# Moving one of two 31-tap convolutions from VectorE to GpSimd, in a two-block transformer kernel

## The reference

```python
hl = modulate(rmsnorm(xl, g_pre_mix[i]), ml[0], ml[1])
zl = hl @ w_in[i]
...
def conformer_branch(z, dw_w, dw_b, ln_g, ln_b):
    a, g = jnp.split(z, 2, axis=-1)
    u = a * jax.nn.sigmoid(g)
    u = depthwise_conv(u, dw_w) + dw_b      # 31 taps, 256 channels, padding 15 on both sides
    u = layernorm(u, ln_g, ln_b)
    return jax.nn.silu(u)
...
merged = jnp.concatenate([rmsnorm(attn, ...), rmsnorm(conf, ...), rmsnorm(sc, ...)], axis=-1)
return merged @ w_o
```

## Time and profile before

| | |
|---|---|
| median of 3 runs | 1858.12 us (1856.57 to 1863.64) |
| the profiled execution, its own time | 1859.7 us |
| its span, first to last instruction | 1857.9 us |
| busy: PE, PEld | 1657.9 us (89%), 1433.6 us (77%) |
| busy: DVE, ACT, POOL | 1235.8 us (67%), 486.9 us (26%), 469.3 us (25%) |
| POOL's hi splits (L1925) | 364 of 128x1024, mean 1291 ns |
| DVE's taps of the two convolutions (L1697) | 120, 84.1 us |

### The profile page before, as it was taken

How to read it: one execution, slowest core, us unless ns; L and a number is a source line. 1 busy time by engine, 2 the same in 40 slices (tenths; PEclk the granted TensorE clock), 3 DMA queues, 4 the chain that set the end, 5 groups by cost and what they waited for, 6 DMA issues and landing times.

```text
span 1857.9 us, 27002 instructions
## 1 busy us (share of the span) xinstructions
PE 1657.9 (89%) x10974; PEld 1433.6 (77%) x10974; DVE 1235.8 (67%) x1668; ACT 486.9 (26%) x1009; POOL 469.3 (25%) x368
## 2 busy tenths in 40 slices
PE   6889589999787899999887979999999797889997
PEld 6876379999687799998654748888888485679996
DVE  7752358887677788868975364444444697568886
ACT  3323212111350412213246251111011513641111
POOL 2200124443232344422200301212121040124442
PEclk9989799999898899999899989999999898989999
DMA  7445655555464555554200203232323041035651
GB/s 263 144 148 167 236 202 174 180 180 181 159 222 164 193 179 181 175 178 159 91 23 1 81 21 114 91 102 90 102 90 101 23 135 58 31 95 177 180 176 54
DMA packets 69876, 247.28 MB, mean 133 GB/s; under 512 B 7456, under 2 KB 10528, under 8 KB 69664
## 3 DMA queue, kind: packets, MB, share of 16 engines
q1 hardware_dynamic: 69792, 246.18, 41.2%
HBM read 245.10 MB, written 1.05 MB: 132 GB/s over the span
## 4 chain that ended last, share of the span: by engine, by line
PE 56%; DVE 31%; ACT 6%; issue 6%; POOL 1%; DMA 0%; SPq 0%; DVEq 0%; POOLq 0%; ACTq 0%
PE psum L319 12%; PE psum L321 12%; PE psum L320 12%; DVE lo_ring L294 9%; DVE relu L1125 4%; DVE c_conf L1697 3%; DVE hid_lo L1126 3%; PE psum L335 3%; PE psum L337 2%; PE psum L336 2%; PE psum L953 2%; DVE x L1088 1%; PE psum L409 1%; POOL hi_ring L1925 1%; DVE normed L1086 1%
## 5 line engine op out<-in xcount | busy, mean ns | idle before, releaser
L1925 POOL TENSOR_SCALAR hi_ring<-raw_ring 128x1024 fp32r<-128x1024 f32 x364 | 469.1, 1291 | 1362.1 <-PE psum L321 674.0
L294 DVE TENSOR_TENSOR lo_ring<-raw_ring,hi_ring 128x1024 fp32r<-128x1024 f32 x364 | 545.8, 1501 | 92.6 <-POOL hi_ring L1925 59.8
L319 PE MATMUL psum<-x_hi,hi_ring 128*128 128x256 f32 (+1 forms) x1424 | 448.2, 315 | 24.1 <-DVE lo_ring L294 24.0
L320 PE MATMUL psum<-x_lo,hi_ring 128*128 128x256 f32 (+1 forms) x1424 | 442.6, 311 | 0.0
L321 PE MATMUL psum<-x_hi,lo_ring 128*128 128x256 f32 (+1 forms) x1424 | 442.4, 311 | 0.0
L319 PE MATMUL psum<-hid_hi,hi_ring 128*128 128x256 f32 (+1 forms) x1024 | 315.8, 308 | 4.1 <-DVE hid_lo L1126 4.1
L321 PE MATMUL psum<-hid_hi,lo_ring 128*128 128x256 f32 (+1 forms) x1024 | 313.7, 306 | 0.0
L320 PE MATMUL psum<-hid_lo,hi_ring 128*128 128x256 f32 (+1 forms) x1024 | 312.7, 305 | 0.0
L319 PEld LDWEIGHTS psum<-x_hi,hi_ring 128*128 128x128 f32 x1424 | 276.2, 194 | 44.3 <-DVE lo_ring L294 30.1
L320 PEld LDWEIGHTS psum<-x_lo,hi_ring 128*128 128x128 f32 x1424 | 276.2, 194 | 13.4 <-issue 0.2
L321 PEld LDWEIGHTS psum<-x_hi,lo_ring 128*128 128x128 f32 x1424 | 275.8, 194 | 13.1
(11 more groups left out here) (373 smaller groups left out, 1889.5 us busy)
## 6 DMA issues: line engine op xcount, KB each, us to landing
raw_ring<-weights SPq DMA_DIRECT2D x460, 512.0 KB, 4.1
h_const<-hyb_consts SPq DMA_DIRECT2D x1, 1088.0 KB, 11.6
x<-xT SPq DMA_DIRECT2D x1, 1024.0 KB, 5.8
x<-ctxT SPq DMA_DIRECT2D x1, 1024.0 KB, 17.1
outT<-x SPq DMA_DIRECT2D x1, 1024.0 KB, 4.8
shared<-shared_consts SPq DMA_DIRECT2D x1, 398.0 KB, 13.8
par<-params SPq DMA_DIRECT2D x1, 301.5 KB, 6.4
```

The source lines that it names most:

```text
L294: nc.vector.tensor_tensor(lo_ring[:, u % SPLIT_SLOTS, :], raw_ring[:, UNIT_AT[u] % RAW_SLOTS, :], hi_ring[:, u % SPLIT_SLOTS, :].bitcast(F ...
L319: nc.tensor.matmul(bank(u % BANKS, T), w_hi, hi[:, k, 0:T], start=(k == 0), stop=False)
L320: nc.tensor.matmul(bank(u % BANKS, T), w_hi, lo[:, k, 0:T], start=False, stop=False)
L1925: nc.gpsimd.tensor_scalar(hi_ring[:, u % SPLIT_SLOTS, :], raw_ring[:, slot, :], 1.0, 0.0, ALU.mult, ALU.add).then_inc(hi_ready, 1)
```

## The change

Plane 1's taps leave DVE and go to POOL, in both layers; plane 0 and the third branch stay. [...] POOL first rounds all units up to base+7, waits until DVE has written plane 1 of `c_u`, and then does three taps, one hi split, three taps, and so on, until the 31 are done: ten groups of three, and one of a single tap. DVE takes 3 taps a unit in place of 5 or 4, and 2 after each of the last three lo splits in place of 6. Waits are added: DVE's for its own memset of the pads, and PE's "mean" and DVE's "center" wait for `pool_taps`.

```diff
+    c_tap = r("c_tap", [P, 2, TB])
...
+    POOL_TAPS = [3, 3]
...
             if step == "mean":
                 pe.wait_ge(flag("branches_done"), l + 1)
+                pe.wait_ge(flag("pool_taps"), l + 1)
...
-        link(nc.vector.memset(c_u[:, :, :, PAD + SEQ:], 0.0))
+        nc.vector.memset(c_u[:, :, :, PAD + SEQ:], 0.0).then_inc(flag("pads_set"), 1)
+        dve.wait_ge(flag("pads_set"), l + 2)
...
-                    taps.extend((conf_tap, i, k) for k in range(CONF_K))
+                    taps.extend((conf_tap, i, k) for k in range(CONF_K if i == 0 else 0))
...
-                do_taps(4 if l else 5)
+                do_taps(3)
...
             if step == "center":
                 dve.wait_ge(flag("conf_mean_ps"), l + 1)
+                dve.wait_ge(flag("pool_taps"), l + 1)
...
+            do_taps(2)
+            if i == 2:
                 branch_dve("taps")
-            do_taps(6)
...
+            def tap(L, j):
+
+                T, S = L.T, L.S
+                parts = lambda ap: ap.rearrange("p (s t) -> p s t", s=S)
+                acc, source = parts(c_conf[:, 1, 0:T]), c_u[:, 1, 0:S, j:j + SEQ]
+                w = pcol("conf_w", (2 * L.l + 1) * CONF_K + j)
+                if j == 0:
+                    link(nc.gpsimd.tensor_scalar(acc, source, w, pcol("conf_b", 2 * L.l + 1), ALU.mult, ALU.add))
+                    return
+                product = parts(c_tap[:, j % 2, 0:T])
+                link(nc.gpsimd.tensor_scalar(product, source, w, None, ALU.mult))
+                last = nc.gpsimd.tensor_tensor(acc, product, acc, ALU.add)
+                if j < CONF_K - 1:
+                    link(last)
+                else:
+                    last.then_inc(flag("pool_taps"), 1)
+
+            u = 0
+            for L in LAYERS:
+                a1 = L.base + ORDER.index("a1")
+                while u <= a1 + SPLIT_SLOTS:
+                    hi_split(u)
+                    u += 1
+                wait_drained(pool, a1)
+                j = 0
+                while j < CONF_K:
+                    for _ in range(min(POOL_TAPS[L.l], CONF_K - j)):
+                        tap(L, j)
+                        j += 1
+                    hi_split(u)
+                    u += 1
+            while u < UNITS:
+                hi_split(u)
+                u += 1
```

More of the change, by code:

```diff
@@ L253, in program @@
     consts_set, split_hi, x_ready = sem("consts_set"), sem("split_hi"), sem("x_ready")
-    pe_step, act_step, dve_step = sem("pe_step"), sem("act_step"), sem("dve_step")
+    pe_step, act_step, dve_step, pool_step = sem("pe_step"), sem("act_step"), sem("dve_step"), sem("pool_step")
     flags = {}
@@ L1919, in _, with hi_split @@
         def _(pool):
-            for u in range(UNITS):
+            link = Link(pool, pool_step)
+            def hi_split(u):
                 slot, turn = UNIT_AT[u] % RAW_SLOTS, UNIT_AT[u] // RAW_SLOTS
```

## The result

| | before | changed |
|---|---|---|
| median | 1859.87 us (4 runs, 1856.57 to 1863.64) | 1928.79 us (4 runs, 1927.2 to 1930.4) |
| ratio | | 1.0353, 95% interval 1.0332 to 1.0375 |
| span of the profiled execution | 1857.9 us | 1926.6 us |

The change makes the kernel 3.5% slower, 66 us by the ratio, 68.9 us between the medians and 68.7 us between the two spans. The forecast was 1902 us (+44) with a range from 1857 to 1932. The direction and the path were right, the size was a third too small.

A forecast was written before the change was run, and what follows sets the result against it. PE was taken to set the pace in layer 0's input projection, DVE just keeping up, with waits for `c_kl` before the kv units. 27 (layer 0) + 20 - 3 (layer 1) = 44 us on 1858.1 gave 1902 us, range 1857 to 1932.

The forecast's parts named there:

- The path: Input projection: hi splits queued behind three POOL taps delay base+16's lo split, `c_kl` and the kv unit, through nine groups.
- POOL's price of a tap: Product, addition and two waits on POOL: 1.85 us a tap in layer 0, 1.15 us in layer 1.
- Rival C: POOL dearer than thought (weight from memory, wait for itself, two inputs through one port): 1930 to 1960 us; chance 0.11.
- Contention: DVE instructions in POOL's way, each at full time less 0.2 us: 26.1 us in layer 0, 18.5 in layer 1.
- The sum in layer 0: POOL alone 59.5 us plus 26.1 of DVE in its way; kv unit at 947 instead of 920.0, +27 us.
- What comes back in layer 1: Leftover taps behind `rotate(0)` go, ahead of the first maximum: -3 us.
- The clock: PE's granted clock falls in its pauses, mostly beside POOL's and DVE's pace: nothing added, some 5 us at the upper end.
- Rival A: POOL and DVE run side by side, so no exclusion time is added: 1857 us, no change; chance 0.10.
- B: Faster: POOL and DVE side by side and low prices, a 4.2 us group, PE setting the pace: 1843 us; chance 0.07.
- D: Cheap POOL taps with the exclusion between POOL and DVE as it is: 1864 to 1880 us; chance 0.12.

The follow-up runs named there:

- experiment 4: The changed kernel with one POOL tap ahead of each hi split from base+8 to base+20 and the other 18 behind them; a single execution took 1928.6 us.
- experiment 1: The changed kernel with POOL's product in six forms by tap number (constant or memory weight, one or two operations, flat operands); a single execution took 1920.8 us.
- experiment 2: The changed kernel without 30 of plane 0's 31 taps on DVE, left out in each layer; a single execution took 1920.0 us.
- the cheap form: The changed kernel with a second operation, + 0.0, in every product on POOL; 1911.1 us, ratio 1.0251 to the kernel before.

## Why the prediction came out as it did

**The path** (a hi split behind three taps, the lo split of base+16, `c_kl`, the kv unit): right, and shown by experiment 4, where it is relieved and PE's wait moves to the mean. POOL had no pause, PE waited for six lo splits in layer 0 (up to 5.8 us each), there was no wait for `pool_taps` in the changed kernel: all as forecast. DVE's 30 taps in layer 0 took 1.11 us each on average, where I had named 1.2 or more.

**POOL's price of a tap** is the term that failed. I had 1.85 us in layer 0; it is 3.0 (the row at 888.89). Of the difference 1.0 us is the product: 1.56 for my 0.6, outside even the upper bound of 1.06 that I had taken from the hi split as the nearest row. It is not of the same kind; it does two operations, and the product one (experiment 1). The addition is 1.26 us for my 1.05; the estimate from the Trainium skill ("GPSIMD Engine Reference", section 3.1), 1.12, was nearer, and 0.14 low. In layer 1 a tap takes 1.8 us (0.92 + 0.72 and two waits) for my 1.15. Rival C, dearer for an unknown reason, got 0.11 and named causes of which the one that was real, the missing second operation, was not one. All prices are those of a product and an addition apart; whether POOL can do both in one instruction no run here tried.

**Contention** was oversized. The ninth hi split ends at 960.85 us, 102.3 us after POOL's first tap began. 26 taps of 3.02 (78.5), nine hi splits (9.5) and about 1 us for the first tap leave 13 us of waiting for DVE (an estimate from these rows), where I had added 26.1. (A slip in that sum, 27 taps of 0.66 us as 18.1 for 17.8, doesn't matter.) I had charged every DVE instruction its full time less 0.2 us. That is right for the lo splits (1.07 of 1.14 us), but not for the taps (0.5 us for three in experiment 2), which fall beside a slow product. Even with the cheap form it is 2.0 us a group, not 2.9.

**The sum in layer 0**: 89 - 59.5 = +30 us on POOL, 13 - 26 = -13 us of contention, together +17, and the kv unit came at 963.3 for my 947. In layer 1 the nine groups took 69.2 us (1540.48 to 1609.66) for my 59.1, and the kv unit was 29.7 us late for my 20. By the same estimate that is +17 us on POOL (26 taps of 1.83, nine hi splits and a first tap of 0.6) and -7 us of contention. The two errors had opposite signs. With the measured prices and my contention the sum would have been some 1947 us, outside the range. So that the range held is luck; the path and the sign are not.

**What comes back in layer 1**: I had 3 us, it is 4.8 us to the maximum (29.7 - 24.9) and 1.8 more to the end. **The clock**: as forecast it fell while PE was waiting anyway; I had added nothing for it, and in the shadow of POOL's groups it cost nothing. Behind the kv unit layer 0 grew by another 2.4 us (45.6 - 43.2). Of these, 1.7 appear at one place: a maximum of the scores at 1008.72 is 42.6 us late and the next one, at 1015.98, 44.3 us, with a granted clock of 0.91 in the 20 us from 999.4 and of 1.00 in the same stretch before (956.8 to 976.8). That the clock is their cause is likely, and no run isolates it.

**Rival A** (side by side) fell by the products at 881.22 and, in experiment 2, at 877.15, each longer by about the lo split in its way. What it had hoped for, another behaviour of instructions with two inputs, isn't there either. An addition on POOL beside DVE's copy into `c_K`, in the changed kernel:

```profile
910.42 3.21 POOL L1946 TENSOR_TENSOR c_conf<-c_tap,c_conf 128x512 f32<-128x512 f32 x1
```

```profile
909.77 2.71 DVE L1754 COPY c_K<-c_kr 32x4096 f32<-32x4096 f32 x1
```

It took 3.21 us for 1.26. **B** (faster) needed A and a group of 4.2 us; the group is 11.7. **D** (cheap taps) could not come about, since the addition and the two waits alone take 1.4 us a tap; even in the cheap form the loss is 2.5%.

## What to carry to other kernels

An engine's low busy share says nothing about whether a stage has room: ask what else is queued on it there, who waits for that, and what the share is in that stretch. Two engines that exclude each other, as these did in the traces here, are one resource for such work. An instruction of 0.66 us on DVE became two of 0.70 and 1.26 us on POOL, and DVE lost 1.5 us to them: such a move can pay only if the work keeps the other engine out for less time than it took there. And a row of "the same operation" bounds a price only if it is the same form, second operation included; where none is there, measure the new instruction by itself before building on it.

## What the runs showed of the hardware that was not expected

- On POOL a tensor_scalar with one operation takes 1.56 us for 128x512 float32 and 0.92 us for 128x256; with a second operation, + 0.0, it takes 0.62 and 0.40 us (constants), or 0.69 and 0.48 us at the least seen with the weight from memory. In the slow form a constant factor or flat operands change little (1.69 and 1.98 us on average, DVE's share included).
- A tensor_tensor on POOL takes 1.26 us for 128x512 and 0.72 us for 128x256, 2.1 ns an element.
- The wait of a POOL instruction for the one just before it costs 0.08 to 0.1 us.
- The exclusion between POOL and DVE doesn't cost both the same: a lo split on DVE holds a POOL product up by its full length (2.63 for 1.56 us), while DVE's taps cost POOL 0.5 us in three beside products of 1.56 us.
